# Hymba layer with a 64-expert MoE on one core: the first group of input weights in two transfers, the norm's weights on another queue, the second x transposed one step earlier

## The chip, the cores and the metric

The kernel is one launch on one core of a Trainium2 chip. The metric is the device time of that launch in microseconds. Before the change it is 1495.38 us, the median of 3 runs (1491.60 to 1497.11).

Names: TensorE (PE) multiplies matrices and transposes through its array, with the loads of its stationary operand recorded apart (PEld); VectorE (DVE), ScalarE (ACT) and GpSimd (POOL) compute elementwise; SyncE (SP) only issues DMAs. DMAs are issued here from SP's queue (q1, "hardware_dynamic") and from POOL's queue (q0, "software_dynamic"). SBUF has 128 partitions; TensorE writes to PSUM.

## The reference

One decoder layer over x of 1024 tokens x 1024 channels, float32:

```
u    = rms_norm(x) * mix_norm_w
proj = u @ w_in                      # 1024 x 2304: columns b | c | h | q | k | v
y_c  = b * causal_dwconv3(c * h)
y_a  = sliding-window attention(q, k, v)  # window 128, ALiBi, sinks, QK norm
x    = x + concat(rms_norm(y_c), rms_norm(y_a)) @ w_out
xn   = rms_norm(x)
x    = x + routed experts(xn)        # 64 experts, 8 per token, group-limited
         + shared expert(xn)
```

The change touches only the first lines of this for the first two of eight row tiles: the norm of x, its product with `mix_norm_w`, and `u @ w_in`.

## The kernel before

The tokens are worked in eight tiles of 128 rows (`tiles[0]` to `tiles[7]`). All five engines run programs of their own, written out by hand in order, and wait on semaphores; nothing is scheduled by a planner. So the order on an engine is the order of the code, and the order of data on SP's queue is the order of its `dma_start` calls.

For a tile T the way into the projection is:
- SP loads x into `x_sb` (`load_x`, L386).
- TensorE transposes it in eight 128x128 pieces into `psT` (`t_x`, L731 to 738). It multiplies by no norm yet.
- ScalarE sums the squares of x (L1100), VectorE makes mean plus eps (L1310), POOL takes the power -0.5 (L548).
- VectorE multiplies `psT` by the norm's weights `mixw`, one per channel, into `uT` (`read_uT`, L1353). For a tile after the first it waits until all projections of the tile before have read `uT`.
- TensorE multiplies `uT` by the columns of `w_in`, group by group (`project`, L740 to 752). The order is `GROUPS` (L312): c, h, b, q (512 columns each), then kv (256 columns), each over eight steps of 128 channels (`k`). A float32 matmul shows in the trace as two records, so a group of eight steps is 16 records.
- ScalarE scales what it reads from `psP` by the norm (L1123). The two banks of `psP` alternate.

`w_in` stays in SBUF as `[128 partitions, 8 steps, 2304 columns]` (in `wts`). SP loads it group by group (L389 to 393), each of 2 MB in pieces of 2 KB, kv 1 MB in pieces of 1 KB, with a semaphore per group (`win_ld`). After the third group SP waits until POOL has made its constants (`s_const_pool` 15), then issues q, kv, the second x, `w_out` (4 MB) and the third x.

`mixw` (L105) holds `mix_norm_w` as 128 partitions x 8: 1024 single elements of 4 bytes. It is the first DMA of POOL (L537). POOL then makes the identity matrix for the transposes (L539 to 543), the power for the first tile, and issues eleven loads of constants (L554 to 563: norm weights, sinks, `convw` of 768 KB, `ffnw` of 512 KB, router bias, router weights of 256 KB), the larger ones broadcast to all partitions.

TensorE's program starts with `t_x(tiles[0])`, the five groups of tile 0, `t_x(tiles[1])`, and then the steps of `front` (L838 to 880), each of which works the attention of one tile, the projections of the next and the router of the one before. From about 430 us on it does the experts, in a loop over jobs of 128 rows.

Of the kernel before, what the change touches and what calls it, by code (L numbers as in the profile page):

```python
# [20 lines left out]
P = 128  # L21
# [13 lines left out]
def hymba_moe(nc, x, mix_norm_w, w_in, conv_w, q_norm_w, k_norm_w, sinks, conv_out_norm_w, attn_out_norm_w,  # L35
# [16 lines left out]
    KT = D // P  # L52
# [18 lines left out]
    with ExitStack() as ctx:  # L71
        def sb(name, shape, dt=F32):
            return ctx.enter_context(nc.sbuf_tensor(name, shape, dt))

        def sem(name):
            return ctx.enter_context(nc.semaphore(name))
# [15 lines left out]
        w_in_sb = wts[:, 0:WIN].rearrange("p (k n) -> p k n", k=KT)  # L92
# [12 lines left out]
        mixw = sb("mixw", [P, KT])  # L105
# [112 lines left out]

        s_const_ld = sem("const_ld")
        s_mixw_ld = sem("mixw_ld")  # L220
        s_const_pool = sem("const_pool")
        s_const_dve = sem("const_dve")
        s_wout_ld = sem("wout_ld")
# [81 lines left out]
        win_ld = [sem(f"win_ld_{g}") for g in ("c", "h", "b", "q", "kv")]  # L305
# [6 lines left out]
        GROUPS = [("c", DC, DC), ("h", 2 * DC, DC), ("b", 0, DC), ("q", 3 * DC, DA), ("kv", 3 * DC + DA, 2 * DKV)]  # L312
        NGR = len(GROUPS)
# [4 lines left out]
        tiles = [Tile(t) for t in range(NT)]  # L318
# [65 lines left out]
        def _(sp):  # L384
            def load_x(T):
                sp.dma_start(x_sb[:, T.buf], x2[T.rows, :]).then_inc(x_ld[T.buf], 16)  # L386

            load_x(tiles[0])
            for g, (_, c0, n) in enumerate(GROUPS):  # L389
                sp.dma_start(w_in_sb[:, :, c0:c0 + n], w_in[0].rearrange("(k p) n -> p k n", p=P)[:, :, c0:c0 + n]) \  # L390
                  .then_inc(win_ld[g], 16)
                if g == 2:
                    sp.wait_ge(s_const_pool, 15)
# [121 lines left out]
            n = sp.value_load(n_jobs[0:1, 0:1], min_val=MIN_JOBS, max_val=JMAX)  # L515
# [17 lines left out]
        def _(pool):  # L533
            def const(dst, src):
                pool.dma_start(dst, src, allow_slow_non_contiguous=True).then_inc(s_const_ld, 16)

            pool.dma_start(mixw[:, :], mix_norm_w[0].rearrange("(k p) -> p k", p=P),  # L537
                           allow_slow_non_contiguous=True).then_inc(s_mixw_ld, 16)
            nc.gpsimd.memset(minus_half[:, :], -0.5).then_inc(s_const_pool, 1)  # L539
            nc.gpsimd.memset(ident[:, :], 0.0).then_inc(s_const_pool, 1)  # L540
            pool.wait_ge(s_const_pool, 2)
# [173 lines left out]
            n = pool.value_load(n_jobs[0:1, 0:1], min_val=MIN_JOBS, max_val=JMAX)  # L715
# [11 lines left out]
        def _(pe):  # L727
            def mm(out_, lhsT, rhs, start, stop):
                return nc.tensor.matmul(out_, lhsT, rhs, start=start, stop=stop)  # L729

            def t_x(T):  # L731

                pe.wait_ge(x_ld[T.buf], T.use * 16)
                if T.t == 1:
                    pe.wait_ge(s_uT_ready, 1)
                for k in range(KT):
                    i = nc.tensor.transpose(psT[:, k, :], x_sb[:, T.buf, k * P:(k + 1) * P], ident[:, :])  # L737
                i.then_inc(s_tx, 1)

            def project(T, g, ks=range(KT)):  # L740

                _, c0, n = GROUPS[g]
                bank = (NGR * T.t + g) % 2
                if 0 in ks:
                    if g == 0:
                        pe.wait_ge(s_uT_ready, T.t + 1)
                    if T.t or g >= 2:
                        pe.wait_ge(s_proj_out, T.t * NGR + (g - 1))
                for k in ks:
                    i = mm(psP[:, bank, 0:n], uT[:, k, :], w_in_sb[:, k, c0:c0 + n], k == 0, k == KT - 1)  # L750
                if KT - 1 in ks:
                    i.then_inc(s_proj, 1)
# [228 lines left out]

            pe.wait_ge(s_const_pool, 3)
            t_x(tiles[0])
            for g in range(NGR):
                pe.wait_ge(win_ld[g], 16)
                project(tiles[0], g)
            t_x(tiles[1])
            pe.wait_ge(s_const_ld, 16 * N_CONST)
            front(step)

# [89 lines left out]
            n = pe.value_load(n_jobs[0:1, 0:1], min_val=MIN_JOBS, max_val=JMAX)  # L1080
# [14 lines left out]
        def _(act):  # L1095
# [6 lines left out]
            def read_group(T, g):  # L1102
                name, _, n = GROUPS[g]
                bank = (NGR * T.t + g) % 2
                dst = {"c": c_sb, "h": h_sb, "b": b_sb, "q": q_sb}.get(name)
                if name == "kv":
                    dst = kv_sb[:, T.par, :]
                if g == 0:
                    act.wait_ge(s_x_rms, (T.t + 1) * 2)
                if T.t:  # L1110
                    if name == "c":
                        act.wait_ge(s_conv, T.t * 6)
                        act.wait_ge(s_u_st, T.t * 16)
                    if name == "h":
                        act.wait_ge(s_u_ready, T.t)
                    if name == "b":
                        act.wait_ge(s_conv, T.t * 6)
                    if name in "qkv":
                        act.wait_ge(s_qk_norm, T.t * 8)
                    if name == "kv":  # L1120
                        act.wait_ge(s_pv, T.t)
                act.wait_ge(s_proj, T.t * NGR + g + 1)
                A(dst, psP[:, bank, 0:n], ACT.Copy, scale=st_x[:, 2:3]).then_inc(s_proj_out, 1)  # L1123
# [692 lines left out]
```

## Time and profile before

| | before |
|---|---|
| median of 3 runs | 1495.38 us |
| the profiled execution | 1495.03 us |
| its span, first to last instruction | 1493.2 us |
| mean granted TensorE clock | 0.999 |
| TensorE busy | 1471.5 us (99%), 6687 matmuls |
| VectorE busy | 660.0 us (44%) |
| ScalarE busy | 299.4 us (20%) |
| GpSimd busy | 665.9 us (45%) |
| DMA | 330.06 MB, mean 221 GB/s |

A busy TensorE is the bound over nearly the whole span; what is left are the places where it waits. Time in a view is counted in us from the start of the span. In a timeline row the first number is the start, the second the duration, and the bracket the idle time of that engine before it with what ended it. In the DMA views "x MB, y%" of a queue is what it moved in the stretch and the time of its packets as a share of 16 engines' time; the sum over queues can pass 100%. The last number of an issue row is the time from issue to landing.

### The profile page before, as it was taken

The numbers are of one execution on the slowest core, as the hardware profiler recorded it, in microseconds if no ns is written. First come the engines' busy times: TensorE is split into PE (matmuls) and PEld (weight loads), VectorE is DVE, ScalarE is ACT, GpSimd is POOL, SyncE is SP. The second block draws the span as 40 slices with busy tenths as digits, with TensorE's granted clock in tenths as the row PEclk, the third lists the DMA queues.
The fourth block names the chain that finished last, engine by engine and source line by source line (L and its number), as shares of the span: only waits on it lengthen the run. The fifth ranks groups of instructions, "written<-read, shape, count | busy, mean of one in ns | idle before, by whom it ended". The sixth has DMA issues, their size and how long they took to land.

```text
span 1493.2 us, 24086 instructions
## 1 busy us (share of the span) xinstructions
PE 1471.5 (99%) x6687; PEld 651.1 (44%) x6688; DVE 660.0 (44%) x890; ACT 299.4 (20%) x568; POOL 665.9 (45%) x626
## 2 busy tenths in 40 slices
PE   7999999999999999999999999999999999999998
PEld 3556556566565433333333333333333333333333
DVE  2343444354355454444444444444444444444432
ACT  1223323323323201111111111111111111111110
POOL 3010221212302525556665566555666556666541
PEclk9999999999999999999999999999999999999999
DMA  9511201201155569999998998888899898998937
GB/s 345 194 53 36 78 29 50 78 15 64 52 232 201 165 261 289 301 289 306 292 352 261 314 284 260 255 263 248 267 350 344 276 321 269 298 296 255 329 56 212
DMA packets 74493, 330.06 MB, mean 221 GB/s; under 512 B 14631, under 2 KB 16168, under 8 KB 48788
## 3 DMA queue, kind: packets, MB, share of 16 engines
q1 hardware_dynamic: 44996, 249.62, 45.3%
q0 software_dynamic: 29456, 79.93, 22.8%
q8 instruction: 22, 0.36, 0.1%
q14 instruction: 19, 0.16, 0.0%
HBM read 282.74 MB, written 65.11 MB: 233 GB/s over the span
## 4 chain that ended last, share of the span: by engine, by line
PE 94%; DMA 3%; DVE 1%; issue 1%; ACT 0%; SPq 0%; DVEq 0%; POOL 0%; POOLq 0%; ACTq 0%
PE psP L729 55%; PE psW L729 30%; PE psT L888 5%; DMA area<-x_dram 1%; DMA wts<-in_w_in_dram 1%; PE psW L951 1%; PE psW L780 1%; PE psT L822 0%; PE psT L806 0%; PE psT L737 0%; DMA out_dram<-area,sidx 0%; PE psW L757 0%; DMA x_dram<-area,sidx 0%; DVE area L1419 0%; DVE st_s L1429 0%
## 5 line engine op out<-in xcount | busy, mean ns | idle before, releaser
L729 PE MATMUL psP<-wts,bias 128*64 (+1 forms) x1296 | 575.7, 597 | 1.2 <-issue 1.1
L729 PE MATMUL psP<-area,bias 128*64 128x512 f32 x1264 | 561.0, 597 | 0.0
L729 PE MATMUL psW<-wts,area 128*64 (+2 forms) x1592 | 426.1, 592 | 1.6 <-DVE wts L1652 1.1
L729 PEld LDWEIGHTS psP<-wts,bias 128*64 128x64 f32 (+1 forms) x1296 | 172.9, 138 | 338.4 <-issue 338.4
L685 POOL DMA_INDIRECT out_dram<-area,sidx x79 | 172.5, 2184 | 287.5 <-ACT area L1246 203.6
L729 PE MATMUL psP<-wts,area 128*128 128x512 f32 (+1 forms) x704 | 287.6, 559 | 6.2 <-DMA wts<-in_w_in_dram 4.9
L685 POOL DMA_INDIRECT x_dram<-area,sidx x79 | 249.0, 3151 | 24.1 <-issue 24.1
L729 PEld LDWEIGHTS psW<-wts,area 128*64 128x64 f32 (+1 forms) x1592 | 149.7, 147 | 250.6 <-issue 249.1
L1652 DVE COPY wts<-wts 128x2048 f32 x79 | 97.0, 1228 | 299.0 <-issue 299.0
L1644 DVE COPY area<-wts 128x4096 f32 x79 | 181.3, 2294 | 25.3 <-issue 21.6
L729 PEld LDWEIGHTS psP<-wts,area 128*128 128x128 f32 x704 | 130.9, 191 | 136.3 <-issue 126.2
L729 PEld LDWEIGHTS psP<-area,bias 128*64 128x64 f32 x1264 | 167.0, 137 | 0.0
L1226 ACT ACTIVATE dsq<-psP 128x256 f32<-128x256 f32 x87 | 33.4, 384 | 567.7 <-PE psP L729 567.7
L1616 DVE SCALAR_TENSOR_TENSOR dsq<-dsq,area,psP 128x256 f32<-128x256 f32 x79 | 53.0, 671 | 180.2 <-ACT dsq L1226 180.2
L1246 ACT ACTIVATE area<-psW 128x1024 f32<-128x1024 f32 x79 | 81.0, 1026 | 253.3 <-PE psW L729 182.4
L662 POOL DMA_INDIRECT area<-xn_dram,gidx x75 | 78.7, 1050 | 69.7 <-POOL gidx L659 63.8
L1609 DVE COPY bias<-psT 128x1024 f32<-128x1024 f32 x79 | 96.1, 1217 | 3.5 <-PE psT L888 3.4
L888 PEld LDWEIGHTS psT<-ident,area 128*128 128x128 f32 x632 | 67.8, 140 | 65.0 <-issue 65.0
L548 POOL TENSOR_TENSOR st_y<-st_y,minus_half 128x1 f32<-128x1 f32 x16 | 8.9, 557 | 182.4 <-DVE st_y L1310 182.4
L888 PE MATMUL psT<-ident,area 128*128 128x128 f32 x632 | 86.3, 280 | 1.8 <-DVE bias L1609 1.8
L615 POOL DMA_INDIRECT slot_table<-pay,slot_i x64 | 62.6, 978 | 21.4 <-issue 19.1
L548 POOL TENSOR_TENSOR st_q<-st_q,minus_half 128x10 f32<-128x10 f32 x8 | 15.7, 1967 | 108.0 <-DVE st_q L1310 108.0
(222 smaller groups left out, 870.1 us busy)
## 6 DMA issues: line engine op xcount, KB each, us to landing
wts<-in_w_exp_gate_dram SPq DMA_DIRECT2D x64, 1024.0 KB
wts<-in_w_exp_up_dram SPq DMA_DIRECT2D x64, 1024.0 KB
wts<-in_w_exp_down_dram SPq DMA_DIRECT2D x64, 1024.0 KB, 6.9
wts<-in_w_in_dram SPq DMA_DIRECT2D x4, 2048.0 KB, 18.0
area<-in_x_dram SPq DMA_DIRECT2D x8, 512.0 KB
wts<-in_w_out_dram SPq DMA_DIRECT2D x1, 4096.0 KB, 18.3
area<-u_dram SPq DMA_DIRECT2D x16, 256.0 KB, 2.9
xn_dram<-area POOLq DMA_DIRECT2D x8, 512.0 KB
```

The costliest lines, as they stand in the source:

```text
L548: nc.gpsimd.tensor_tensor(out_, in_, minus_half[:, 0:n], ALU.pow).then_inc(sem_, 1)
L615: pool.indirect_dma_start(out=table[:, :], out_offset=bass.IndirectOffsetOnAxis(ap=slot_i[:, n:n + 1], axis=0), in_=pay[:, t, j, :], in_of ...
L662: pool.indirect_dma_start(out=xg[:, par], out_offset=None, in_=xn_dram[:, :], in_offset=bass.IndirectOffsetOnAxis(ap=gidx[:, par:par + 1], ...
L685: pool.indirect_dma_start(out=(out2, x1_dram)[b][:, :], out_offset=bass.IndirectOffsetOnAxis(ap=sidx[b][:, par:par + 1], axis=0), in_=ysb[ ...
L729: return nc.tensor.matmul(out_, lhsT, rhs, start=start, stop=stop)
L888: i = nc.tensor.transpose(psT[:, k, :], xg[:, par, k * P:(k + 1) * P], ident[:, :])
L1226: A(sg, psP[:, par, 0:FE], ACT.Silu).then_inc(s_silu, 1)
L1246: A(ysb[:, par], psW[:, 2:4, :].rearrange("p a n -> p (a n)"), ACT.Copy).then_inc(s_y_ready, 1)
L1609: V.tensor_copy(xT[par], psT[:, :, :]).then_inc(s_xT_ready, 1)
L1616: V.scalar_tensor_tensor(out=hh.rearrange("t (f p) -> t p f", f=FT), in0=sg.rearrange("t (p f) -> t p f", f=FT), scalar=w, in1=psP[:, par, ...
L1644: V.tensor_copy(gu_b[par].rearrange("p m k f -> p m (k f)"), wts[:, bass.ds((e % NSLOT) * SLOTW, 2 * GUW)].rearrange("p (m n) -> p m n", m ...
L1652: V.tensor_copy(dn_b, wts[:, bass.ds((e % NSLOT) * SLOTW + 2 * GUW, FT * D)]).then_inc(s_dn_copy, 1)
```

## The change

Three edits:
- SP loads `mixw`, right behind the first x; POOL no longer does.
- The first group (c) comes in two transfers, the k-steps 0 to 3 and 4 to 7, each 1 MB, with a semaphore for the first half (`s_win_half`). TensorE projects the first four steps after the first half and the other four after the second.
- TensorE transposes the second x ahead of the fifth group (kv) instead of behind it.

```diff
@@ SP
             load_x(tiles[0])
+            sp.dma_start(mixw[:, :], mix_norm_w[0].rearrange("(k p) -> p k", p=P),
+                         allow_slow_non_contiguous=True).then_inc(s_mixw_ld, 16)
+            _, c0, n = GROUPS[0]
+            sp.dma_start(w_in_sb[:, 0:KT // 2, c0:c0 + n],
+                         w_in[0].rearrange("(k p) n -> p k n", p=P)[:, 0:KT // 2, c0:c0 + n]).then_inc(s_win_half, 16)
+            sp.dma_start(w_in_sb[:, KT // 2:KT, c0:c0 + n],
+                         w_in[0].rearrange("(k p) n -> p k n", p=P)[:, KT // 2:KT, c0:c0 + n]).then_inc(win_ld[0], 16)
             for g, (_, c0, n) in enumerate(GROUPS):
+                if g == 0:
+                    continue
@@ POOL
-            pool.dma_start(mixw[:, :], mix_norm_w[0].rearrange("(k p) -> p k", p=P),
-                           allow_slow_non_contiguous=True).then_inc(s_mixw_ld, 16)
@@ TensorE
             t_x(tiles[0])
-            for g in range(NGR):
+            pe.wait_ge(s_win_half, 16)
+            project(tiles[0], 0, range(0, KT // 2))
+            pe.wait_ge(win_ld[0], 16)
+            project(tiles[0], 0, range(KT // 2, KT))
+            for g in range(1, NGR):
+                if g == NGR - 1:
+                    t_x(tiles[1])
                 pe.wait_ge(win_ld[g], 16)
                 project(tiles[0], g)
-            t_x(tiles[1])
```

SP's first DMAs, before (a row gives the line, what is written and read, the shape, and the semaphores waited for; `area` holds x):

```order
L386 DMA area<-in_x_dram 128x1024
L390 DMA wts<-in_w_in_dram 128x8x512 x3
L390 DMA wts<-in_w_in_dram 128x8x512 [waits const_pool]
L390 DMA wts<-in_w_in_dram 128x8x256
L386 DMA area<-in_x_dram 128x1024
```

And now, in the changed kernel, whose line numbers are other ones:

```order
L387 DMA area<-in_x_dram 128x1024
L390 DMA mixw<-in_mix_norm_w_dram 128x8x1
L393 DMA wts<-in_w_in_dram 128x4x512
L395 DMA wts<-in_w_in_dram 128x4x512
L400 DMA wts<-in_w_in_dram 128x8x512 x2
L400 DMA wts<-in_w_in_dram 128x8x512 [waits const_pool]
L400 DMA wts<-in_w_in_dram 128x8x256
L387 DMA area<-in_x_dram 128x1024
```

`mixw` stands in front of all weights on this queue, and c is two rows of four k-steps.

TensorE from its first group to the second tile, before (`win_ld_c` and the like are the groups' semaphores, `x_ld2` the second x):

```order
L729 MATMUL psP<-wts,area 128x512 [waits uT_ready,win_ld_c]
L729 MATMUL psP<-wts,area 128x512 x7
L729 MATMUL psP<-wts,area 128x512 [waits win_ld_h]
L729 MATMUL psP<-wts,area 128x512 [waits proj_out,win_ld_b]
L729 MATMUL psP<-wts,area 128x512 [waits proj_out,win_ld_q]
L729 MATMUL psP<-wts,area 128x256 [waits proj_out,win_ld_kv]
L729 MATMUL psP<-wts,area 128x256 x7
L737 MATMUL psT<-ident,area 128x128 [waits uT_ready,x_ld2]
L737 MATMUL psT<-ident,area 128x128 x7
L729 MATMUL psP<-wts,area 128x512 [waits proj_out,uT_ready,const_ld]
```

And now:

```order
L737 MATMUL psP<-wts,area 128x512 [waits uT_ready,win_half]
L737 MATMUL psP<-wts,area 128x512 x3
L737 MATMUL psP<-wts,area 128x512 [waits win_ld_c]
L737 MATMUL psP<-wts,area 128x512 [waits win_ld_h]
L737 MATMUL psP<-wts,area 128x512 [waits proj_out,win_ld_b]
L737 MATMUL psP<-wts,area 128x512 [waits proj_out,win_ld_q]
L745 MATMUL psT<-ident,area 128x128 [waits uT_ready,x_ld2]
L745 MATMUL psT<-ident,area 128x128 x7
L737 MATMUL psP<-wts,area 128x256 [waits proj_out,win_ld_kv]
L737 MATMUL psP<-wts,area 128x256 x7
L737 MATMUL psP<-wts,area 128x512 [waits proj_out,uT_ready,const_ld]
```

The first group has two waits, and the eight transposes stand between q and kv. (Rows that only finish a group are left out in both.)

## Rows read from the trace of the kernel before

**Rows 1.** The chain that ended last, 0 to 60 us: start, us, what.
```profile
1.23 0.42 SPq L390
...
1.70 18.88 DMA wts<-in_w_in_dram
...
20.62 24.32 PE psP L729 x64
44.94 0.87 PE psT L737 x8
45.81 1.36 issue
```

**Rows 2.** DMA issues at 1.23 us and at 2.32 us: size, us to landing.
```profile
wts<-in_w_in_dram SPq DMA_DIRECT2D x1, 2048.0 KB, 9.6
...
wts<-in_w_in_dram SPq DMA_DIRECT2D x1, 2048.0 KB, 24.6
```

**Rows 3.** Timeline of SP's queue, the issue of b.
```profile
2.32 4.33 SPq L390 DMA_DIRECT2D wts<-in_w_in_dram  x1
```

**Rows 4.** Timeline of TensorE, 4 to 21 us.
```profile
4.47 1.94 PE L737 MATMUL psT<-ident,area 128*128 128x128 f32 x8 [4.47 <-DMA area<-in_x_dram]
10.86 9.34 PE L729 MATMUL psP<-wts,area 128*128 128x512 f32 x16 [4.44 <-DMA wts<-in_w_in_dram]
20.62 0.70 PE L729 MATMUL psP<-wts,area 128*128 128x512 f32 x1 [0.42 <-DMA wts<-in_w_in_dram]
```

**Rows 5.** Queues: 0:10, 0:15, 15:19 (q1), 15:20 us (both).
```profile
q1 hardware_dynamic: 1173, 2.62, 74.0%
...
q1 hardware_dynamic: 1976, 4.24, 81.9%
...
q1 hardware_dynamic: 248, 0.49, 33.1%
...
q0 software_dynamic: 296, 1.32, 65.0%
q1 hardware_dynamic: 330, 0.65, 34.7%
```

**Rows 6.** Queues around the load of mixw: 4:6, 6:8, 8:10 (q1), 6:7 us (q0).
```profile
q1 hardware_dynamic: 386, 0.79, 103.1%
...
q1 hardware_dynamic: 206, 0.42, 57.3%
...
q1 hardware_dynamic: 379, 0.76, 101.8%
...
q0 software_dynamic: 17, 0.00, 87.4%
```

**Rows 7.** DMA packets: 22:26 us (2 KB), 38:44 us (4 KB), q1 21:27 us.
```profile
DMA packets 770, 1.55 MB, mean 388 GB/s; under 512 B 12, under 2 KB 12, under 8 KB 770
...
DMA packets 598, 2.45 MB, mean 408 GB/s; under 512 B 0, under 2 KB 0, under 8 KB 598
...
q1 hardware_dynamic: 1117, 2.25, 102.1%
```

**Rows 8.** Timeline of VectorE, 0 to 10 us.
```profile
8.69 1.22 DVE L1353 TENSOR_TENSOR area<-psT,mixw 128x1024 f32<-128x1024 f32 x1 [2.99 <-DMA mixw<-in_mix_norm_w_dram]
```

**Rows 9.** Timeline of ScalarE and VectorE, 41 to 46 us.
```profile
41.52 0.69 ACT L1123 ACTIVATE area<-psP,st_x 128x512 f32<-128x512 f32 x1 [6.18 <-PE psP L729]
...
45.85 1.23 DVE L1353 TENSOR_TENSOR area<-psT,mixw 128x1024 f32<-128x1024 f32 x1 [16.55 <-PE psT L737]
```

**Rows 10.** Timeline of TensorE's weight loads in group c.
```profile
14.43 0.34 PEld L729 LDWEIGHTS psP<-wts,area 128*128 128x128 f32 x1 [0.52 <-issue]
...
16.18 0.19 PEld L729 LDWEIGHTS psP<-wts,area 128*128 128x128 f32 x1 [0.24 <-issue]
```

**Rows 11.** Stretch 12 to 14 us: busy us (x), then PEclk, DMA share, GB/s.
```profile
12.00:14.00 2.00, 2.00 (x4) 0.88 (x3) 0.00 (x0) 0.00 (x0) 1.93 (x9) 1.00 0.95 314
```

**Rows 12.** Timeline of TensorE, a group of 16 at 83 us.
```profile
83.55 7.03 PE L729 MATMUL psW<-wts,area 128*128 128x512 f32 x16
```

More of the change, by code:

```diff
@@ L220, in hymba_moe @@
         s_mixw_ld = sem("mixw_ld")
+        s_win_half = sem("win_half")
         s_const_pool = sem("const_pool")
```

## The prediction

> **What bounds the kernel now.** I read the page first: TensorE is busy 99% of the span (the table above). The work on it is not touched by the change, which only reorders the first 50 us. So the question is what TensorE waits for there, and the view to read next is the chain of waits over the first 60 us [rows 1]. The reader is to see one DMA piece in it, from 1.70 to 20.58, then TensorE without a break until 45.8, a pause of 1.36 us, and TensorE again. The 18.88 us DMA piece is not the first group of weights (c) but the second (h): c was issued at 1.23 and took 9.6 us to land [rows 1, 2], so it was there at 10.8; the transfer issued at 1.70 is h.
>
> Then the timeline of TensorE [rows 4]. Its c matmuls start at 10.86, last 9.34 us and end at 20.20; h starts at 20.62, 0.42 us later. Group c ends just as h arrives: TensorE waits 4.44 us for DMA before c and 0.42 us before h. That is what decides this change: whatever moves c forward moves only c, and the time comes back as idle time ahead of h unless h lands earlier too. The most that can be had is read off from here, and so is the term that matters, the landing of h.
>
> What sets it is in the DMA views by stretch. x (0.52 MB), c (2.10) and h (2.10) make 4.72 MB on SP's queue, whose transfers land in order (c 10.8, h 20.6, b 26.9 [rows 1 to 3]). That queue (q1) had moved 2.62 MB at 10 us and 4.24 MB at 15 us [rows 5]: h was 0.48 MB short. Then the constants from POOL's queue (q0) come in with 65% of the engines' time and q1 moves only 0.65 MB in 5 us, 0.49 of it in the first four [rows 5]. So the last half megabyte of h takes 4 us, and a shortfall at 15 us costs about three times what it would elsewhere: 0.12 to 0.16 MB per us there, against 0.79 MB in 2 us at full rate [rows 6].
>
> **The change part by part.**
>
> Two transfers for c. The bytes and the packets (2 KB each) are the same, on the same queue. TensorE may start on four of eight k-steps when 1.57 MB have moved. By [rows 5, 6] the queue stood at 2.62 - 0.76 - 0.42 = 1.44 MB at 6 us, so at full rate that is at 6.3; c's landing came 0.8 us after its bytes (10.8 against 10.0), so the first half would land at 7.1 with nothing ahead of it. SP spends one more issue of 0.42 us [rows 1]. Its cover is deep: h is needed in the queue at 10 us, and b's issue already stood 4.33 us for room in the queue, until 6.65 [rows 3], and behind it SP only waits for POOL's constants.
>
> The Trainium skill (DMA: Bandwidth & Descriptors, Rules for kernel authors) speaks against such a cut: each transfer carries a fixed cost, and it wants one large transfer. The trace does not show that cost between queued transfers: q1 keeps 102% of the engines' time from 21 to 27 us, over the border between b and q [rows 7]. By the page's fixed cost of about 2 us a transfer the sum would, as an estimate, be up to 2 us longer; by the row nothing.
>
> The norm's weights on SP. This is 4 KB in 1024 elements of 4 bytes, 64 for each of 16 engines. On POOL's queue it took 17 packets (one holds all 64 of an engine) and 87.4% of 16 engines for 1 us: 14.0 us / 1024 = 13.7 ns an element, 0.87 us an engine [rows 6]. Around it q1 moved 0.42 MB in 2 us instead of 0.79: 0.37 MB lost, and I count all of it as given back by the change, which is generous: POOL's packets had passed after the first of the two. On SP's queue the trace has no 4-byte elements, but it has packet prices: 83.1 ns for 2 KB (4 us x 16 / 770) and 160.5 ns for 4.1 KB (6 x 16 / 598) [rows 7], from which a packet costs 8 ns beside its bytes. I take 13.7 + 8 = 22 ns for an element that is a packet by itself: 64 x 22 = 1.4 us an engine, in order ahead of c and h, or 0.55 MB at 0.395 MB per us. Bounds: nothing at all, and 83.1 ns (as a 2 KB packet), 5.3 us.
>
> What that does to h: at 15 us the queue stands at 4.24 + 0.37 - 0.55 = 4.06 MB, 0.66 short. [Rows 5] give 0.65 MB by 20 us, so h's bytes are through at 20.1 instead of 19.0: h lands 1.1 us later, at 21.7. Lower bound (elements free): 0.11 short, through at 16.0, landed by 17.6. Upper bound: 1.73 MB behind before, 3.3 MB at 21 us (at 0.16 MB per us in the last), the remaining 1.4 MB at 2.25 MB in 6 us [rows 7], through at 24.7, landed at 26.3: 5.7 us later.
>
> What it does to c: the norm's weights now land behind x, no longer just ahead of 8.69; VectorE's multiply, which waited 2.99 us for them [rows 8], takes its place right behind the transposes (end 6.41) [rows 4]: 6.45 + 1.22 = 7.7. The first half lands at 7.1 + 1.4 = 8.5. c then runs from 8.6 for 9.34 us to 17.9; its second half (1.05 MB, 2.7 us later) has landed by 11.2, when TensorE is at its third k-step at most. So c ends 2.3 us earlier, and TensorE waits 3.8 us for h instead of 0.42. POOL saves an issue, but its next step that counts, the power for x's norm, waits for x, and its constants are issued behind that: as before, worth 0.
>
> The second x transposed ahead of kv. Before: kv ends at 44.94, the transposes at 45.81, VectorE copies from 45.85 for 1.23 us, TensorE restarts at 47.17 [rows 1, 9]. The copy needs both kv and the transposes done, and their sum is the same in either order: 0. The transposes' x must have landed by the end of q; q ended at 41.5 [rows 9]; up to this x the queue carries 10.5 MB, and from 4.9 MB at 20 us that is done before 35 at the rates of [rows 7]. ScalarE's read of kv now begins 0.9 us later, but ends within VectorE's copy, so the norm of q and k behind that copy is not late. I take 0 and keep 0.2 us either way.
>
> After h nothing waits: b landed at 2.32 + 24.6 = 26.9 [rows 2, 3], needed at 20.62 + 6.9 = 27.5, and moves by half a microsecond when h moves by one. From there to the end TensorE is the chain.
>
> Sum against the profiled execution: 1495.03 (span 1493.2) + 1.1 = 1496.1. The median of the runs shown is 0.35 above it: 1496.5.
>
> **The clock.** The matmuls of c ran at two paces: weight loads 0.86 us apart until 15.29, 0.43 after (a row's own time and the idle time before it) [rows 10], in the first case after 4.4 us without work. The ratio is that of the two levels, 1.2 and 2.4 GHz; the granted clock of the profile says 1.00 from 12 to 14 us too, where the pace was the low one [rows 11], so the pace is the evidence. A group of 16 at full pace takes 7.03 us [rows 12]: the low level cost c 9.34 - 7.03 = 2.3 us. That is no part of the sum as c does not bound. But the change puts 3.8 us of idle time ahead of h, where there were 0.42.
>
> **Rivals.** First, the low clock returns at h and costs the same 2.3 us: 1498.8. For it: the gap of 4.4 us after the transposes was followed by the low pace. Against: there the engine had not yet been at the high one, and after the pause of 1.36 us it came back at 0.43. Chance 0.22. The Trainium skill (TensorE: Matmul & The Clock Gate, HAM oscillation) says that waiting for DMAs between bursts of matmuls brings the half-rate clock back; this case's trace has no wait of such length after full pace.
>
> Second, h lands as before or earlier, because the small elements cost SP's queue less than the 0.37 MB they took out before. With free elements c starts at 7.8, ends at 17.1, and h is there by 17.6, against 20.6: up to 3.0 us, 1492.4. It decides below 14.6 ns an element (0.37 MB at 0.395 MB per us is 0.94 us). For it: 13.7 ns on POOL's queue. Against: the 8 ns a packet. Chance 0.25, mean 1494.5. The Trainium skill (DMA: Bandwidth & Descriptors, Issuing engines are not separate DMA queues) says that whoever issues, the same 16 engines do the work, and only issue time is saved. By that h stays at 20.6 and the time at 1495.4.
>
> Third, slower: each 4-byte element holds SP's queue like a packet of weights, all weights stand behind 64 of them, and the constants then catch h with a megabyte missing. Price up to 5.7 us, with the low clock 8.0: 1501.1 to 1503.4. It decides from about 40 ns an element (2.6 us an engine). For it: the queue is served in order, so nothing passes them; against: 13.7 ns measured. Chance 0.14.
>
> Fourth, nothing is gained or lost because c never bound: that is inside the forecast.
>
> **Numbers.** Forecast (h 0 to 2 us later at full clock, 1495.4 to 1497.5) 0.39, the three rivals 0.22, 0.25, 0.14. The range takes in the first two rivals and the near part of the third, and the spread of the runs of before (1491.6 to 1497.1): 1492.3 to 1500.5. What one can tell from no change here is 0.5%, 7.5 us. No case reaches 7.5 us to the faster side; only the third with the low clock comes to the other. Faster 0.02, same 0.93, slower 0.05.
>
> **What would show it.** c's matmuls start between 8 and 9.5; the norm's weights have landed by 6.5; a wait of 3 to 4 us for DMA stands before the first h matmul, which starts at 21 to 22.5, with loads 0.43 apart behind it; the pause after kv remains near 1.3 us; everything after has the old length. I am wrong in the step on the queue if h starts before 20.5 or after 23, in the step on the clock if loads after h's start are 0.86 apart, and in the last part if the pause after kv and the transposes shrinks or grows by over 0.3 us.

## The result, and the profile after

The changed kernel takes 1496.20 us, the median of 22 runs (1494.99 to 1503.71). The kernel before, run beside it, takes 1493.86 us, the median of 22 (1491.60 to 1497.73). The ratio is 1.0022 with a 95% interval of 1.0015 to 1.0029: slower by 3.3 us (2.2 to 4.3), within the 0.5% that were called no change. (The two medians alone lie 2.3 us apart, near the lower end of that interval.) The profiled execution took 1497.54 us, its span 1495.8.

The forecast was 1496.5, and the time is 0.3 us from it, but that closeness is partly luck. The forecast put its 1.1 us on top of the median of 3 runs (1495.38), which lay 1.5 us above the median of 22. The loss is three times the forecast's 1.1 us.

First the chain that ended last in the changed kernel, 0 to 60 us (start, us, what); it answers to [rows 1].

```profile
2.87 19.89 DMA wts<-in_w_in_dram
...
22.81 22.56 PE psP L737 x48
45.37 0.88 PE psT L745 x8
46.24 3.46 PE psP L737 x16
49.70 1.43 issue
51.13 5.39 PE psP L737 x12
```

The DMA piece is again h, issued at 2.87 and landed at 22.76. Then h, b and q as one row of 48 matmuls, the moved transposes, kv, and the second tile at 51.13, where it was 47.18. So 3.95 us are lost by there. The timeline of TensorE splits them:

```profile
4.16 1.94 PE L745 MATMUL psT<-ident,area 128*128 128x128 f32 x8 [4.16 <-DMA area<-in_x_dram]
9.34 8.84 PE L737 MATMUL psP<-wts,area 128*128 128x512 f32 x16 [3.24 <-DMA wts<-in_w_in_dram]
22.81 22.56 PE L737 MATMUL psP<-wts,area 128*128 128x512 f32 x48 [4.63 <-DMA wts<-in_w_in_dram]
```

Group c starts 1.5 us earlier than in [rows 4], as meant, and ends near 18.2. Then TensorE is idle for 4.63 us where it was idle for 0.42. Group h starts 2.19 us later. The 48 matmuls behind it take 22.56 us. In the runs below that start h behind a short wait or none (e3, e7, e9) they take 20.87; so 1.69 us of it is pace. The pause after kv is 1.43 against 1.36. The sum is 2.19 + 1.69 + 0.07 = 3.95.

The pace is seen in the timeline of the weight loads behind the start of h (those of c are in [rows 10]):

```profile
23.62 0.34 PEld L737 LDWEIGHTS psP<-wts,area 128*128 128x128 f32 x1 [0.51 <-issue]
24.47 0.34 PEld L737 LDWEIGHTS psP<-wts,area 128*128 128x128 f32 x1 [0.52 <-issue]
...
26.75 0.19 PEld L737 LDWEIGHTS psP<-wts,area 128*128 128x128 f32 x1 [0.24 <-issue]
27.18 0.19 PEld L737 LDWEIGHTS psP<-wts,area 128*128 128x128 f32 x1 [0.24 <-issue]
```

They are 0.86 apart until 26.2 and 0.43 from 26.8 on. Here the granted clock agrees, unlike in [rows 11]: in the stretch from 24 to 26 us it is 0.50, the lower level of 1.2 GHz (columns as there):

```profile
24.00:26.00 2.00, 2.00 (x3) 0.68 (x2) 0.00 (x0) 0.00 (x0) 0.00 (x0) 0.50 1.05 385
```

Now the DMA side: the packets and SP's queue in the stretches 3:4 and 4:5 us, then the queue over 5:8 and 0:15, and both queues over 15:20.

```profile
DMA packets 699, 0.17 MB, mean 175 GB/s; under 512 B 657, under 2 KB 657, under 8 KB 699
q1 hardware_dynamic: 699, 0.17, 78.8%
...
DMA packets 425, 0.05 MB, mean 55 GB/s; under 512 B 399, under 2 KB 399, under 8 KB 425
q1 hardware_dynamic: 425, 0.05, 41.0%
...
q1 hardware_dynamic: 537, 1.08, 96.5%
...
q1 hardware_dynamic: 2921, 4.02, 81.8%
...
q0 software_dynamic: 324, 1.37, 67.9%
q1 hardware_dynamic: 337, 0.67, 35.2%
```

The norm's weights are 1056 small packets, nearly all one element each, where POOL's queue took 17 [rows 6]. In those 2 us the queue moves 0.22 MB; before it moved 0.72 (profile of before, 3:5 us). It is not only that the elements are work: the engines are 79% and 41% busy. At 5:8 it gets back 1.08 - 0.83 = 0.25 MB, since POOL's load is gone. At 15 us it stands at 4.02 MB, against 4.24 in [rows 5].

VectorE's multiply now follows the transposes, as was said, and its wait of [rows 8] is gone:

```profile
6.21 1.23 DVE L1366 TENSOR_TENSOR area<-psT,mixw 128x1024 f32<-128x1024 f32 x1 [0.83 <-PE psT L745]
```

The two profiled executions differ by 2.5 us, not by 3.95, because of things that the change doesn't touch. One is the first routed job of the experts. The chain of before:

```profile
526.36 1.08 issue
527.44 8.71 PE psP L729 x32
536.15 3.43 PE psW L729 x16
```

and of after:

```profile
529.35 0.99 issue
530.34 7.09 PE psP L737 x32
537.42 3.43 PE psW L737 x16
```

The same 32 matmuls took 8.71 us in the one and 7.09 in the other. The granted clock in before's stretch from 527 to 533 us is 0.72. Of the profiles below e1, e2, e5, e6, e9 and e11 had the slow first job (8.60 to 10.01 us), e3, e4, e7, e8, e10 and e12 not (7.09). This goes with none of the edits, but each kernel has one profile, the changed one two, so that it is chance from run to run is argued and not shown. It stands behind two waits of TensorE, 1.8 and 1.0 to 1.1 us long, in both.

### The profile page after: what moved, and what is told of

Its sections match the earlier page's. It is cut to its first block, busy times and chain, and to the rows that moved or that the text cites. A ratio compares the mean times of both kernels' runs of the same rounds, so it can differ in the third digit from the quotient of the medians.

```text
span 1495.8 us, 24087 instructions
## 1 busy us (share of the span) xinstructions
PE 1471.3 (98%) x6687; PEld 651.1 (44%) x6688; DVE 659.9 (44%) x890; ACT 299.6 (20%) x568; POOL 663.2 (44%) x625
## 4 chain that ended last, share of the span: by engine, by line
PE 97%; DMA 1%; DVE 1%; issue 1%; DVEq 0%; SPq 0%; ACT 0%
PE psP L737 56%; PE psW L737 31%; PE psT L896 5%; DMA wts<-in_w_in_dram 1%; PE psW L959 1%; PE psW L788 1%; PE psT L830 0%; PE psT L814 0%; PE psT L745 0%; PE psW L765 0%; DVE area L1432 0%; DVE st_s L1442 0%; DVE area L1499 0%; DVE bias L1622 0%; DVE area L1795 0%
```

## The experiments

All ratios are to the kernel before on the same chip, with a 95% interval, from 8 to 12 runs of each variant. "Second tile" is the start of the second tile's first matmul in the variant's profile (47.18 before, 51.13 after). The diffs are shortened: bare names and `...` stand for the full calls.

**e1: c in two transfers, nothing else.**

```diff
@@ before: SP
+  w_in_sb[:, 0:4, c] .then_inc(s_win_half, 16)
+  w_in_sb[:, 4:8, c] .then_inc(win_ld[0], 16)
@@ before: TensorE
+  wait s_win_half; project(tiles[0], 0, range(0, 4))
+  wait win_ld[0];  project(tiles[0], 0, range(4, 8))
```

> Only the split of c, on the kernel before. Theory (h's landing and the clock set the front, the split only moves c): the first half lands at 7 to 8, c starts at about 10.0, when VectorE's product is ready, ends at about 19.3, and h starts at 20.6 as before, at the high pace (idle about 1.3 us). Second tile's first matmul at 47.2 +- 0.4, time as before within 1.5 us. Rival (the cut itself costs, a fixed cost for each transfer): h starts 1 to 2 us later, at 21.6 to 22.6, and the time grows by as much.

Ratio 0.9998 (0.9988 to 1.0008). From its timeline of TensorE:

```profile
10.09 9.10 PE L737 MATMUL psP<-wts,area 128*128 128x512 f32 x16 [3.90 <-DVE area L1365]
20.71 24.32 PE L737 MATMUL psP<-wts,area 128*128 128x512 f32 x64 [1.52 <-DMA wts<-in_w_in_dram]
```

With the norm's weights on POOL's queue c waits for VectorE, no longer for weights, starts 0.77 us earlier, and the time stands as idle time ahead of h: 1.52 for 0.42. h is 0.09 later and at full pace. By itself the cut is free and worth nothing.

**e2: the norm's weights on SP, nothing else.**

```diff
@@ before: SP, behind the first x
+  sp.dma_start(mixw, mix_norm_w) .then_inc(s_mixw_ld, 16)
@@ before: POOL
-  pool.dma_start(mixw, mix_norm_w) .then_inc(s_mixw_ld, 16)
```

> Only the norm's weights on SP behind x, on the kernel before. Theory: all of the loss on the queue is here. h starts at 22.3 to 23.1 instead of 20.62, though c starts at about 11.0 to 12.4 and ends by 21.5; the idle time ahead of h is under 2.5 us, so the clock stays high and the loss is about 2.2 us (ratio 1.0015), less than the whole change's 3.9 us at the second tile's first matmul. Rival (the loss comes from the cut or from the number of transfers): h starts at 20.6 and the time is as before.

Ratio 1.0011 (1.0000 to 1.0023).

```profile
12.87 8.66 PE L729 MATMUL psP<-wts,area 128*128 128x512 f32 x16 [6.61 <-DMA wts<-in_w_in_dram]
22.44 24.32 PE L729 MATMUL psP<-wts,area 128*128 128x512 f32 x64 [0.91 <-DMA wts<-in_w_in_dram]
```

h starts 1.82 us later, and the second tile as well (48.99). This is the part of the loss that comes from the queue. The undivided c is late too, so the wait ahead of h is only 0.91 and h runs at full pace: the second part of the loss did not come with either edit alone.

**e3: the second x transposed ahead of kv, nothing else.**

```diff
@@ before: TensorE
             for g in range(NGR):
+                if g == NGR - 1:
+                    t_x(tiles[1])
                 pe.wait_ge(win_ld[g], 16)
                 project(tiles[0], g)
-            t_x(tiles[1])
```

> Only the second x transposed ahead of kv, on the kernel before. Theory: 0. Last matmul of kv and transposes end together at 45.8 as before, pause 1.36 to 1.45, second tile's first matmul at 47.2 +- 0.2. Rival (kv's later end delays the norm of q and k and with it the second tile): the transposes of q and k start over 0.3 us later behind the second tile's first matmul, or the pause grows by over 0.3 us.

Ratio 1.0003 (0.9992 to 1.0014). h happened to start 0.33 us later in its profile, and the second tile 0.40 later (47.58). The pause is 1.43 for 1.36. The move costs 0.07 us. The rival did not come: the transposes of q and k start 5.23 us behind the second tile's first matmul, 5.22 before.

**e4: the changed kernel with TensorE kept busy ahead of h, first try.**

```diff
@@ after: TensorE, behind the second half of c
+            for _ in range(20):
+                mm(psW[:, 3, 0:P], ident, ident, True, True)
```

> The whole change, with 20 matmuls of the identity by itself (128 columns, float32, into a PSUM bank nobody reads) between c and the wait for h: they occupy TensorE for about 4.3 us of the 4.6 us and compute nothing. Theory of the clock: h still starts at 22.8 +- 0.5, but its weight loads are 0.43 apart from the first, and the second tile's first matmul comes about 1.7 us earlier than in the change, at 49.4 +- 0.5. Rival (the slow pace at h is not from the idle time but from the arrival of data): loads after h's start 0.86 apart for about 3.4 us, second tile at 51.1.

Ratio 1.0035 (1.0023 to 1.0046). The filler ran past the landing of h:

```profile
19.26 4.63 PE L737 MATMUL psW<-ident 128*128 128x128 f32 x40
23.72 20.77 PE L737 MATMUL psP<-wts,area 128*128 128x512 f32 x48
```

h came at full pace but 0.9 us later still than in the changed kernel, and its profile has another 2.1 us of idle time near the end, at 1419.65, that the theory says nothing of. (The second tile, at 50.25, accounts for 3.1 us of loss, a ratio of 1.0021.) As a test of the time it failed. As a test of the pace it was positive: 48 matmuls in 20.8 us. It was built anew as e7.

**e5: the changed kernel with POOL's four large loads of constants held back until h has landed.**

```diff
@@ after: POOL
-            const(convw ...); const(ffnw ...); const(rbias ...); const(wr ...)
@@ after: POOL, behind its last iota
+            pool.wait_ge(win_ld[1], 16)
+            const(convw ...); const(ffnw ...); const(rbias ...); const(wr ...)
```

> The whole change, and POOL's four large constants (convw, ffnw, router bias and weights, 1.56 MB) issued only when h has landed, behind POOL's other constants. Theory (the large constants take two thirds of the DMA engines from 15 us on and stretch the last 0.7 MB of h): q1 moves 0.39 MB per us from 15 us on, h lands at 17.5 to 18.5 instead of 22.8, TensorE goes from c (end 18.2) to h with under 0.5 us idle and at the high pace; second tile's first matmul at 44.5 to 45.5 instead of 51.1, ratio to the kernel before about 0.9985. b is landed by 23 and q by 28. Rival (the constants do not stretch h, the queue's own order does): h lands within 1 us of 22.8, second tile at 50 or later.

Ratio 0.9994 (0.9985 to 1.0004).

```profile
9.44 23.14 PE L738 MATMUL psP<-wts,area 128*128 128x512 f32 x48 [3.13 <-DMA wts<-in_w_in_dram]
33.23 7.13 PE L738 MATMUL psP<-wts,area 128*128 128x512 f32 x16 [0.65 <-DMA wts<-in_w_in_dram]
```

c, h and b run as one row from 9.44: no wait ahead of h is long enough to part them, though the small elements still stand in front. SP's queue moves 1.93 MB from 15 to 20 us where after moved 0.67. h landed at 18.35 (17.5 to 18.5 expected). The second tile starts at 46.12, which is 5.0 us earlier than after, and later than the 44.5 to 45.5 expected, in part because q now waits 0.65 us: from 25 to 30 us the held-back constants move 0.86 MB beside SP's 1.07. So the ratio is short of the 0.9985 expected too.

**e6: the same on the kernel before.**

```diff
@@ before: POOL
+            pool.wait_ge(win_ld[1], 16)  # ahead of the same four loads
```

> Only the late constants, on the kernel before (weights of the norm on POOL, c in one transfer). Theory: h lands at 16.5 to 17.5, but c still starts at 10.86 and ends at 20.2, so that only the 0.42 us ahead of h go: second tile's first matmul at 46.8 +- 0.3, ratio 0.999 to 1.0. Now c bounds. Rival (h's landing is all that counts): second tile at 44 to 45.

Ratio 0.9992 (0.9981 to 1.0002). All 80 matmuls of the first tile run as one row from 10.84, 34.26 us long, and the second tile is where it was (47.33, not the 46.8 expected). The wait of 0.42 us ahead of h is gone, but c's loads stayed 0.86 apart until 16.97, for 15.29 in [rows 10], and that took the gain back. So before the change the constants cost h no more than that wait. In the two pairs of profiles they matter where c starts early (e5 against after) and not where it doesn't (e6 against before).

**e7: the changed kernel with a filler that ends in time.**

```diff
@@ after: TensorE, behind the second half of c
+            for _ in range(4):
+                mm(psW[:, 3, :], ident, x_sb[:, tiles[0].buf, 0:512], True, True)
```

> The whole change with four wide matmuls (identity by x, 512 columns, results unused) in the wait ahead of h, instead of the twenty small ones: 3.4 us of work in eight records, so that the program of TensorE hardly grows. Theory of the clock: h starts at its landing, 22.3 to 23.2, at 0.43 a load, and the second tile's first matmul at 49 to 49.7. Theory of the code: the slow stretch of e4_fill near 1420 us (2.1 us idle and low pace) came from the place at which the longer program is loaded, so it is gone or elsewhere here, and the time lies 1 to 3 us under e4_fill's (ratio 1.0005 to 1.002). Rival (the filling itself costs later): ratio again at 1.003 or more.

Ratio 1.0007 (0.9997 to 1.0016).

```profile
18.95 3.60 PE L737 MATMUL psW<-area,ident 128*128 128x512 f32 x8
22.49 20.87 PE L737 MATMUL psP<-wts,area 128*128 128x512 f32 x48
```

h starts when it did, and the 48 matmuls take 20.87 us. The second tile is at 49.12, 2.0 us before after's. Work that computes nothing takes back 1.5 thousandths of the time. That is the second part of the loss, shown by taking away the idle time alone. The idle time near 1420 us that e4 had is not in this profile; what it comes from stays open.

**e8: the changed kernel once more,** to see what of its profile comes back.

> The changed kernel once more, unchanged. If the 2.56 us of idle time of TensorE at 1452.6 us, beside which both instruction loads of that queue stand at 1451 to 1455, come from the place of the code, they are there again (2 to 3 us before the four psP matmuls behind the loop); if they are chance, this run shows 0.1 us there and 1.1 us ahead of the next psW matmuls as the other kernels do. In the front: h's start at 22.3 to 23.2 and the low pace for 3 to 4 us behind it again, second tile's first matmul at 50.5 to 51.5. Rival for the front: the low pace was chance, and the second tile starts at 49 to 49.6.

Ratio 1.0022 (1.0012 to 1.0033), the same as the first time.

```profile
22.25 23.51 PE L737 MATMUL psP<-wts,area 128*128 128x512 f32 x48 [3.53 <-DMA wts<-in_w_in_dram]
```

The low pace at h is back (23.51 us, 2.64 over full pace). An idle time of 2.56 us at 1452.58 in after's profile, which none of its code explains, is not: there e8 has the usual 1.09 us wait for VectorE. So that one does not belong to the kernel.

**e9: the changed kernel with the norm's weights on ScalarE's queue.**

```diff
@@ after: SP
-            sp.dma_start(mixw[:, :], ...).then_inc(s_mixw_ld, 16)
@@ after: ScalarE, its first instruction
+            act.dma_start(mixw[:, :], ...).then_inc(s_mixw_ld, 16)
```

> The changed kernel, with the norm's weights issued as the first DMA of ScalarE's queue instead of second on SP's; the two transfers for c and the moved transposes stay. Theory (the 1024 four-byte packets hold SP's queue, because each engine works them one after the other ahead of c): on a queue of their own they stand beside the weights, q1 moves 0.9 MB or more from 2 to 5 us (0.53 now, 0.98 before), h's matmuls start within 0.7 us of the 20.6 before, c's by 9.5, the wait ahead of h is under 3 us, and the second tile starts at 47 to 48.5 (51.1 now); ratio to before 0.9985 to 1.001. Rival (the elements cost the 16 engines the same whoever issues them): q1 still moves 0.5 to 0.6 MB from 2 to 5 us, h starts at 22 to 23 behind a wait over 3.5 us, with loads 0.86 apart, second tile 50.5 to 51.5, ratio 1.0015 to 1.003.

Ratio 1.0002 (0.9993 to 1.0011). The queues over 3:5 us:

```profile
q1 hardware_dynamic: 111, 0.27, 45.3%
q10 hardware_dynamic: 1028, 0.00, 27.8%
```

and TensorE:

```profile
8.41 10.01 PE L735 MATMUL psP<-wts,area 128*128 128x512 f32 x16 [1.78 <-DMA wts<-in_w_in_dram]
20.06 20.87 PE L735 MATMUL psP<-wts,area 128*128 128x512 f32 x48 [1.65 <-DMA wts<-in_w_in_dram]
```

Neither side is wholly right. The elements take as much from the weights while they pass as they do on SP's queue (0.27 MB against 0.22 in the same 2 us), which the rival had said: 27.8% of 2 us on 16 engines by 1028 packets is 8.7 ns each, and the engines are idle for a quarter of the time besides. But SP's queue is back to full rate at once (1.20 MB from 5 to 8 us, where after has 1.08), stands at 4.27 MB at 15 us, and h starts 0.56 us ahead of before and 2.75 ahead of after, at full pace. The times at which the shares of c and h landed, in the table of the next section, show the difference: with the elements on SP's queue some of its shares fall behind, on ScalarE's they don't.

**e10 to e12: towards a faster kernel.** All three have the norm's weights back on POOL's queue and hold the large constants until b, the third group, has landed. e11 adds four filler matmuls ahead of c, and e12 also issues the output weights later.

```diff
@@ e10: after, mixw on POOL, and on POOL behind its last iota
+            pool.wait_ge(win_ld[2], 16)
+            const(convw ...); const(ffnw ...); const(rbias ...); const(wr ...)
@@ e11: also on TensorE, behind t_x(tiles[0])
+            for _ in range(4):
+                mm(psW[:, 3, :], ident, x_sb[:, tiles[0].buf, 0:512], True, True)
@@ e12: also on SP
-            w_out; load_x(tiles[2]); table; zrow
+            table; zrow; load_x(tiles[2]); w_out
```

> The changed kernel with the norm's weights back on POOL's queue, and POOL's four large loads of constants held back until the third group has landed. The two transfers for c and the moved transposes stay. Theory (h is late only through POOL's constants, and through the small elements where they stand on SP's queue): c starts at 10.1, c to q run without a wait over 0.5 us and kv too, at the low pace until about 17, so the second tile starts at 10.1 + 4 x 7.03 + 3.5 + 0.9 + 1.4 + 2.3 to 3.5 for the clock = 46.3 to 47.5; ratio 0.9985 to 1.0. Rival (the constants are now too late: held back, they catch q, kv or the second x): a wait for DMA over 1 us before q, kv or the second tile, start of it over 48, ratio above 1.0.

Ratio 0.9990 (0.9981 to 1.0000), median 1491.66. c to q is one row:

```profile
10.07 29.92 PE L738 MATMUL psP<-wts,area 128*128 128x512 f32 x64 [3.77 <-DVE area L1367]
```

The second tile starts at 45.76, a bit ahead of the 46.3 expected. The low pace ended before 15 us and cost what was expected, 29.92 - 27.63 = 2.3 us; but four groups in one row take 27.63 at full pace (e11 below), not the four times 7.03 of the expectation, since the 7.03 of [rows 12] has the end of a row in it. Nothing else waits; the constants are not too late.

> The run with the constants held back behind the third group and the norm's weights on POOL's queue, plus four matmuls of 512 columns (identity times x, into an unused bank) between the first transposes and c, so that TensorE has work from 4.5 us on; they compute nothing that is used. Theory (the low pace of c is a matter of TensorE's idle time before it, and h is no longer what c waits for): c starts at 10.1 to 10.4 and turns to loads 0.43 apart at least 2 us earlier than in the run without them; second tile 44 to 45.5, ratio 0.997 to 0.9985. Rival (h's landing binds again as soon as c is faster): c ends by 18, a wait of 1 to 2.5 us for DMA stands ahead of h, the second tile starts at 45.8 or later.

Ratio 0.9983 (0.9973 to 0.9992), median 1490.64.

```profile
6.13 5.19 PE L738 MATMUL psW<-area,ident 128*128 128x512 f32 x8
11.16 27.63 PE L738 MATMUL psP<-wts,area 128*128 128x512 f32 x64
```

The filler was slow at first (5.19 us for 8 records) and held c up, which could have started at 10.1. But the low pace is now spent on work that doesn't count; all of c to q is at full pace (27.63 us), and no wait stands ahead of h. Second tile at 44.55.

> As the run with the four filler matmuls, and SP issues the third x and the output weights behind the table's first store and the zero rows instead of ahead of them. Theory (with the second tile early, the zero rows queued behind 4 MB of output weights hold SP until 51.8 and with it the first tile's convolution): the store of u starts by 49, the waits of TensorE between 50 and 100 us that stand in the run without the new order go, and the time is 1 to 2.5 us below it. Rival (the convolution has slack of its own): the two have the same times within 0.5 us, and the same waits of TensorE between 50 and 100 us.

Ratio 0.9985 (0.9976 to 0.9994), median 1490.51. The one wait of 0.7 us that e11 has between 50 and 100 us is gone, as expected, but u, whose store is now issued at 38.14 behind the output weights, is read back at 51.01, for 52.51: the 4 MB are merely ahead of another transfer. The time is e11's, as the rival said. e11 and e12 beat both kernels, by 2.5 us (1.2 to 4.0) the one before in the ratio of e11.

| | c starts | h starts | second tile | ratio |
|---|---|---|---|---|
| before | 10.86 | 20.62 | 47.18 | 1 |
| after | 9.34 | 22.81 | 51.13 | 1.0022 |
| e8, after again | 9.28 | 22.25 | 51.52 | 1.0022 |
| e1, split | 10.09 | 20.71 | 47.27 | 0.9998 |
| e2, norm's weights on SP | 12.87 | 22.44 | 48.99 | 1.0011 |
| e3, transposes | 10.84 | 20.95 | 47.58 | 1.0003 |
| e4, after and long filler | 9.40 | 23.72 | 50.25 | 1.0035 |
| e5, after, constants late | 9.44 | in the row | 46.12 | 0.9994 |
| e6, before, constants late | 10.84 | in the row | 47.33 | 0.9992 |
| e7, after and filler | 9.56 | 22.49 | 49.12 | 1.0007 |
| e9, on ScalarE's queue | 8.41 | 20.06 | 46.69 | 1.0002 |
| e10, constants late | 10.07 | in the row | 45.76 | 0.9990 |
| e11, and filler ahead of c | 11.16 | in the row | 44.55 | 0.9983 |
| e12, and output weights late | 10.85 | in the row | 44.24 | 0.9985 |

The ratio follows the second tile: from 44.55 to 51.13 are 6.6 us, and 0.0039 of 1493.86 are 5.8. In every row but e4's the shift of the second tile lies within the interval of the ratio. e4 loses some 2 us more than its front explains.

## Why the prediction was right or wrong

**What bounds: right.** Moving c forward moved only c. It starts at 9.34 (8 to 9.5 were said), and the gain stands ahead of h, 4.63 us of it where 3.8 were said. e1 has it alone: 0.77 earlier, 1.10 more idle time.

**The cut costs nothing: right.** By the fixed cost of about 2 us a transfer of the Trainium skill (DMA: Bandwidth & Descriptors, Anatomy of one DMA — SWDGE (gpsimd) path) h would, as an estimate, have come up to 2 us later; e1 has 0.09. That figure is a fit to transfers issued by GpSimd, and the prediction used it for SP's. The section that the prediction named beside it (Rules for kernel authors) asks for 1 MiB or more in a transfer, which either half of c has, so the Trainium skill spoke less against this cut than the prediction said.

**The norm's weights on SP's queue: the state of the queue right, the landing of h half as late as it was.** They landed at 1.23 + 4.1 = 5.3 (by 6.5 were said). At 3:5 us 0.50 MB were lost for 0.55 in the sum; 0.25 were given back for 0.37; the queue stood at 4.02 MB at 15 us for 4.06, and moved 0.67 MB by 20 for 0.65. But the two prices in it were wrong in how they are made up: an element is 9 to 10 ns of an engine's time, not 22 (for SP's queue: 119.8% of 16 us in 3:5, less 0.22 MB at 83.1 ns per 2 KB, over 1024), and the rest is engines without work. The step that failed is the last: "h's bytes are through at 20.1 instead of 19.0: h lands 1.1 us later". The sum of the queue passed 4.72 MB at about 20.2 us (4.52 at 19, 0.33 more by 21), as said. h landed at 22.76, 2.6 us behind that, not the 1.6 of before, which I had taken as a constant. In e2 and e8 it is 1.8 and 2.0, in e1 and e3, without elements on SP's queue, 1.3 and 1.5. h was 1.6 to 2.2 us later in three profiles (e2, e8, after), against 1.1.

The traces show what the sum of a queue hides. The semaphore of a transfer is raised in 16 steps, and the time of each is in the trace. I take a step for the share of one of the 16 DMA engines; the trace does not name the engine. In us:

| | elements on | c, first and last step | h, first, 12th, last step |
|---|---|---|---|
| before | POOL's queue | 10.09, 10.81 | 18.61, 19.83, 20.58 |
| e1 | POOL's queue | 10.15, 10.90 | 18.92, 20.29, 20.67 |
| e9 | ScalarE's queue | 10.06, 11.05 | 17.75, 19.13, 20.02 |
| after | SP's queue | 10.26, 12.87 | 18.83, 20.42, 22.76 |
| e2 | SP's queue | 10.51, 12.82 | 19.35, 21.98, 22.39 |
| e8 | SP's queue | 10.50, 12.67 | 19.15, 21.63, 22.20 |

With the elements on SP's queue c's steps lie 2.2 to 2.6 us apart, in all six profiles that have them there (e4, e5 and e7 too), and at most 1.0 us in the other eight. In after twelve shares of h are there by 20.42 and four only from 22.26 on. On the mean the 16 steps are 1.3 us later than in before and 0.7 later than in e1, around the forecast's 1.1; the last is 2.2 later. So, as I read the steps, the elements do not hold all engines equally. The sum had 1.4 us for each engine, and a transfer is there only when its last share is. Why some are held longer stays open. The same holds for the first half of c: twelve of its steps are there by 8.15, the last at 9.29, where 8.5 was forecast.

By the signs given in advance the step would have been wrong from 23 us on; h started at 22.81, and in e8 at 22.25, within the 21 to 22.5 said. So the sign did not catch this.

The second rival, with h as before or earlier, did not come, nor the Trainium skill's rule beside it (DMA: Bandwidth & Descriptors, Issuing engines are not separate DMA queues). By the rule it would be the same whoever issues; the traces have h start at 20.6 to 20.7 with the elements on POOL's queue (before, e1), at 20.06 on ScalarE's (e9) and at 22.3 to 22.8 on SP's (e8, after). The third rival, with a price of up to 5.7 us, did not come either.

**The clock: wrong.** I forecast h at full pace and gave the low clock 0.22. It came, in both profiles of the changed kernel, and cost 1.7 and 2.6 us (2.3 were put down). The reason against it was a pause of 1.36 us after which the pace had stayed. That was evidence for pauses of this length only; the idle time to come was 3.8 by my own sum, and the nearest row to that was the 4.44 in [rows 4], with the low pace behind it. What spoke for the rival was in the rows, and I discounted it because TensorE "had not yet been at the high one". The Trainium skill (TensorE: Matmul & The Clock Gate, HAM oscillation) said what happened, and the trace now agrees: waits of 0.91 to 1.65 us ahead of h (e2, e1, e9) kept the pace, 3.53 and 4.63 (e8, after) lost it. e7, which has h start when the changed kernel does but no idle time ahead of it, kept it too: it is the idle time and not the landing of h.

So the two terms are 2.2 + 1.7 for 1.1 + 0. The rival's 1498.8 less the 1495.38 it was made from is 3.4 (1.1 + 2.3), next to the 3.95 of the profile and the 3.3 of the ratio: the loss is the rival's, and the time came out at the forecast's in part because the base of the forecast was 1.5 us high.

**The second x: right.** 0.07 us in e3 and in after; 0 within 0.2 were said.

**The constants: right in part.** That the last half megabyte goes slowly was the basis, and e5 shows it: held back, they give SP's queue 1.26 MB more in 5 us. I wrote of them only as a given. They are what turns a small shortfall at 15 us into a wait. [Rows 5] also show how they get two thirds: the two queues move nearly as many packets (296 and 330 in 5 us), but POOL's are 4.5 KB on the mean and SP's 2 KB.

## What to carry to other kernels

Before bringing the first of a row of transfers forward, look at which lands last: unless that one comes sooner, the gain becomes idle time further on, and a TensorE idle for some microseconds pays again, in low pace, when it starts. Load small scattered elements on another queue than the weights; hold bulk constants until the weights that are waited for have landed (worth something only where TensorE does wait for them, see e6); and spend the first slow microseconds of TensorE on work that computes nothing. Judge a landing by the last share of its transfer, not by the sum of the queue's bytes.

## What the runs showed of the hardware

- The granted clock can hide the low pace. From 12 to 14 us it is 1.00 in [rows 11] while loads come 0.86 apart; in after it is 0.50 from 24 to 26 us at the same spacing. In the first case TensorE had not yet been at full pace, in the second it had.
- The low pace's price on c differs between runs: loads turn to 0.43 apart 3.5 us after c's first load in after, 4.4 in before [rows 10], 6.0 in e9, and c takes 8.84, 9.34 and 10.01 us. Work just ahead of c brings the change forward, to 9.4 us from the start of the span in e11:

```profile
8.69 0.34 PEld L738 LDWEIGHTS psW<-area,ident 128*128 128x128 f32 x1 [0.52 <-issue]
9.44 0.19 PEld L738 LDWEIGHTS psW<-area,ident 128*128 128x128 f32 x1 [0.42 <-issue]
```

- 1024 elements of 4 bytes are 17 packets when POOL issues them and over 1000 when SP or ScalarE does, yet the weights lose nearly as much: 0.37 MB in [rows 6] and 0.50 and 0.45 in after and e9.
- Small elements ahead of large transfers on one queue part the shares of these transfers: the 16 steps of c lie 2.2 to 2.6 us apart with them and 0.5 to 1.0 without (14 profiles).
- Late in the program, where the loop over jobs ends, some executions have an idle time of TensorE without a releaser: 2.56 us in after and 3.10 in e5, none in e8, the same kernel as after. The chain of a single profile there is no evidence for a variant.
